# Three rounded products for the branch and attention output layers, with a new order of the conv transfers

## The reference

```python
# block 1, first layer: a causal convolution over time, 31 taps per channel
u = a * sigmoid(gate)                       # of h @ w_pw1
u = conv(u, w_dw) + b_dw                    # depthwise
u = silu(layer_norm(u)) @ w_pw2 + b_pw2
# block 2, end: two attentions with 8 heads of 64 each, gated, and two output layers
y_a = o_a * silu(z_a);  y_b = o_b * silu(z_b)
m = sigmoid(gate_a) * (y_a @ w_a) + sigmoid(gate_b) * (y_b @ w_b)     # "branch"
x = x + rms_norm(m @ w_o)                                             # "w_o2"
# block 3, middle: three mixers, each with an output layer, then a common one
merged = sigmoid(g_a) * ya + sigmoid(g_b) * yb + sigmoid(g_c) * yc    # ya, yb, yc: "outs3"
x = x + merged @ w_o                                                  # "w_o3"
```

## Time and profile before

| | |
|---|---|
| runs | 2034.17, 2035.84, 2044.3 us; median 2035.84 |
| profiled execution | 2035.59 us, span 2033.8 us, mean granted clock 0.994 |
| TensorE | 1986.1 us busy, 98% of the span |
| VectorE, ScalarE, POOL | 1494.9, 1187.3, 58.1 us busy |
| DMA | 510.23 MB, mean 251 GB/s; some 370 GB/s in the experts' stage |

### The profile page before, as it was taken

One profiled execution on the slowest core, in us unless ns is written; L12 is line 12 of the kernel. 1 busy time (PEld: TensorE's weight loads), 2 busy tenths in 40 slices (PEclk: granted clock), 3 DMA queues, 4 the chain that ended last, 5 costly groups with the idle time before them and its releaser, 6 DMA issues.

```text
span 2033.8 us, 31638 instructions
## 1 busy us (share of the span) xinstructions
PE 1986.1 (98%) x12238; PEld 1738.0 (85%) x12238; DVE 1494.9 (73%) x1623; ACT 1187.3 (58%) x1264; POOL 58.1 (3%) x105
## 2 busy tenths in 40 slices
PE   8999999999999999999999999999989999999997
PEld 7689999688888888888888888889978879989997
DVE  7766554789989999999899999977484358536652
ACT  4254443778777787777778777773354355325442
POOL 3020000000000000000000000010000000020000
PEclk9999999999999999999999999999999999999999
DMA  6625453399999999999999999974523334445551
GB/s 241 182 104 178 175 196 136 124 359 373 360 372 362 366 371 354 371 365 365 363 366 374 357 372 363 366 272 167 186 84 108 127 116 147 166 145 187 186 183 48
DMA packets 75863, 510.23 MB, mean 251 GB/s; under 512 B 8320, under 2 KB 14464, under 8 KB 14592
## 3 DMA queue, kind: packets, MB, share of 16 engines
q1 hardware_dynamic: 75776, 508.98, 67.4%
HBM read 506.66 MB, written 2.29 MB: 250 GB/s over the span
## 4 chain that ended last, share of the span: by engine, by line
PE 87%; DVE 4%; DMA 3%; issue 2%; ACT 2%; SPq 1%; POOL 0%; ACTq 0%; DVEq 0%; POOLq 0%
PE ps L904 9%; PE ps L908 9%; PE ps L907 9%; PE ps L638 8%; PE ps L641 8%; PE ps L642 8%; PE ps L929 5%; PE ps L933 5%; PE ps L932 5%; PE ps L615 3%; DMA spread<-big 2%; PE ps L1195 2%; PE ps L1198 2%; PE ps L1197 2%; PE ps L1130 1%
## 5 line engine op out<-in xcount | busy, mean ns | idle before, releaser
L1896 DVE TENSOR_TENSOR ring_r<-ring,high 128x2048 fp32r<-128x2048 f32 x227 | 517.6, 2288 | 55.0 <-ACT high L1566 34.0
L1566 ACT ACTIVATE high<-ring 128x2048 fp32r<-128x2048 f32 x224 | 428.8, 1914 | 19.1 <-DMA ring<-w_stream 18.5
L1781 DVE TENSOR_TENSOR ring_r<-ring,high 128x2048 fp32r<-128x2048 f32 x120 | 274.6, 2292 | 128.2 <-ACT high L1379 128.0
L907 PE MATMUL ps<-ring_r,big_r 128*128 128x512 f32 x896 | 349.2, 390 | 0.0
L641 PE MATMUL ps<-scr_r,high 128*128 128x256 f32 (+1 forms) x1200 | 342.7, 286 | 0.0
L1379 ACT ACTIVATE high<-ring 128x2048 fp32r<-128x2048 f32 x120 | 228.2, 1908 | 165.0 <-PE ps L638 93.3
L1896 DVE TENSOR_TENSOR ring_r<-ring,scr_r 128x2048 fp32r<-128x2048 f32 x112 | 256.3, 2288 | 39.6 <-ACT scr_r L1566 39.1
L638 PE MATMUL ps<-sq_r,high 128*128 128x272 f32 (+1 forms) x832 | 238.4, 287 | 5.4 <-DVE scr_r L1788 5.4
L642 PE MATMUL ps<-sq_r,ring_r 128*128 128x272 f32 (+1 forms) x832 | 237.9, 286 | 0.0
L1566 ACT ACTIVATE scr_r<-ring 128x2048 fp32r<-128x2048 f32 x112 | 214.5, 1915 | 22.5 <-DMA ring<-w_stream 22.4
L641 PEld LDWEIGHTS ps<-scr_r,high 128*128 128x128 f32 x1200 | 227.2, 189 | 0.3
(11 more groups left out here) (482 smaller groups left out, 3779.0 us busy)
## 6 DMA issues: line engine op xcount, KB each, us to landing
ring<-w_stream SPq DMA_DIRECT2D x477, 1024.0 KB, 4.8
big<-spread SPq DMA_DIRECT2D x32, 146.0 KB, 2.9
spread<-big SPq DMA_DIRECT2D x8, 151.0 KB, 6.1
h<-h_in SPq DMA_DIRECT2D x1, 1088.0 KB, 5.1
out<-hn SPq DMA_DIRECT2D x1, 1024.0 KB, 4.7
vec<-vec_in SPq DMA_DIRECT2D x1, 576.0 KB, 8.1
```

Of the source, the lines that this page charges most:

```text
L907: pe.matmul(o, x_item_high[:, k, :], w_low[:, cols], start=False, stop=False)
L1566: act.activation(w_high, w, ACT.Copy).then_inc(S["moe_high"], 1)
L1781: dve.tensor_tensor(w_low, blocks_at(c, 0, CH), w_high.bitcast(F32), ALU.subtract).then_inc(S["weights_low"], 1)
L1896: dve.tensor_tensor(w_low, w, w_high.bitcast(F32), ALU.subtract).then_inc(S["moe_low"], 1)
```

## The change

The convolution: each `shift(j)` of all eight now stands before the chunk 6 + j.

Branch, `w_o2` and `w_o3` join the split stages, 4 chunks each, and their matmuls become three rounded products. The gated attention outputs get a rounded part (`gated_high`, ScalarE, over the used gates in `proj_r`) and a low part (`gated_low`, VectorE, in place), one job after `gated`. ScalarE's sigmoids, and the splits of the first two branch chunks on both engines, move into sub 14. POOL's sums now go to `part` and `part3`; ScalarE copies them into `hn_r`, and VectorE makes the low parts two tiles later, in the loop over m. The splits of the remaining chunks lie between these steps.

```diff
@@ convolution, SP
             for c in range(RING, 3 * RING):
-                if c - RING == KD - 2:
-                    shift(KD - 2)
+                if c - RING < KD:
+                    shift(c - RING)
                 sp.wait_ge(pre_begun, c - RING + 2)
                 sp.dma_start(slot(c), w_stream[c]).then_inc(dense_landed[c % RING], 16)
-                if c - RING < KD - 2:
-                    shift(c - RING)
-                if c - RING == KD - 2:
-                    shift(KD - 1)
@@ TensorE, branch
-                        mm = pe.matmul(ps[:, 2 * (j % 2) + 4 * br + half, 0:SEQ], w[:, half * P:half * P + P],
-                                       sq256[:, 4 * br + k, :], start=(k == 0), stop=(k == 3))
+                        mm = pe.matmul(o, w_high[:, cols], proj_r[:, z + k, :], start=(k == 0), stop=False)
                         begun(half == 0 and first, mm)
+                        pe.matmul(o, w_high[:, cols], sq_r[:, 4 * br + k, 0:SEQ], start=False, stop=False)
+                        mm = pe.matmul(o, w_low[:, cols], proj_r[:, z + k, :], start=False, stop=(k == 3))
...
-                    pe.wait_ge(S["y_ready"], 4)
+                    pe.wait_ge(S["input_low"], 8 * 4 + 4)
                     branch(0)
...
-            pe.wait_ge(S["y_ready"], 8)
+            pe.wait_ge(S["input_low"], 8 * 4 + 8)
...
-                pair(BOFF["w_o2"] + j * KD, KD, lambda k: hn256[:, k, :], SEQ, b, S["wo2_done"],
-                     (lambda k: pe.wait_ge(S["br_ready"], k + 1)) if j == 0 else None)
+                split_pair(BOFF["w_o2"] + j * KD, KD, hn_r, in_low, SEQ, b, S["wo2_done"],
+                           after_split(5) if j == 0 else None)
...
-                pair(BOFF["w_o3"] + j * KD, KD, lambda k: hn256[:, k, :], SEQ, b, S["wo3_done"],
-                     (lambda k: pe.wait_ge(S["merged"], k + 1)) if j == 0 else None)
+                split_pair(BOFF["w_o3"] + j * KD, KD, hn_r, merged_low, SEQ, b, S["wo3_done"],
+                           after_split(7) if j == 0 else None)
@@ ScalarE, attention
+            def gated_high(j):
+                act.wait_ge(S["y_ready"], j + 1)
+                whole, high_part, _ = gated_parts(j)
+                act.activation(high_part, whole, ACT.Copy).then_inc(S["input_high"], 1)
...
                     exps(s + 2)
+                if s >= 2 and subs[s - 2][0] != subs[s - 1][0]:
+                    gated_high(subs[s - 2][0])
                 split_weights(chunk2(merge_pairs_done(s) - 1 + LOOK))
-            for p in merge_order:
...
+                if s == len(subs) - 2:
+                    split_weights(BOFF["branch"] // CH + 1)
+                    for p in merge_order:
+                        act.wait_ge(S["in2_dve"], p + 1)
+                        dst, _ = tiles2(p)
+                        act.activation(dst, dst, ACT.Sigmoid).then_inc(S["in2_act"], 1)
+            split_weights(BOFF["branch"] // CH + 2)
+            gated_high(len(jobs) - 2)
+            gated_high(len(jobs) - 1)
+            split_weights(BOFF["branch"] // CH + 3)
             for m in range(KD):
+                act.wait_ge(S["br_ready"], m + 1)
+                act.activation(hn_r[:, m, 0:SEQ], part[:, m % 2, 0, :], ACT.Copy).then_inc(S["input_high"], 1)
+                if m in (1, 3, 5):
+                    split_weights(BOFF["w_o2"] // CH + m // 2)
@@ ScalarE, block 3
             curved(PAIRS3 - 1, ACT.Sigmoid)
+            split_weights(BOFF["w_o3"] // CH + 2)
+            for m in range(KD):
+                act.wait_ge(S["merged"], m + 1)
+                act.activation(hn_r[:, m, 0:SEQ], part3[:, m % 2, 0, :], ACT.Copy).then_inc(S["input_high"], 1)
+                if m == 1:
+                    split_weights(BOFF["w_o3"] // CH + 3)
@@ VectorE, attention
                 while taken2 < merge_pairs_done(s):
                     take2(taken2)
                     taken2 += 1
+                if s == len(subs) - 2:
+                    split_weights(BOFF["branch"] // CH + 1)
+                if s >= 2 and subs[s - 1][0] != subs[s - 2][0]:
+                    gated_low(subs[s - 2][0])
             gated(len(jobs) - 1)
+            gated_low(len(jobs) - 2)
+            gated_low(len(jobs) - 1)
+            split_weights(BOFF["branch"] // CH + 2)
@@ VectorE, branch sums
                 if m >= 2:
-                    dve.wait_ge(S["br_ready"], m - 1)
+                    low_part(in_low[:, m - 2, :], part[:, m % 2, 0, :], hn_r[:, m - 2, 0:SEQ], "input_low")
+                    dve.wait_ge(S["input_low"], 8 * 5 + m - 1)
...
+                if m == 1:
+                    split_weights(BOFF["branch"] // CH + 3)
+                if m in (3, 5):
+                    split_weights(BOFF["w_o2"] // CH + m // 2 - 1)
@@ VectorE, block 3
+            split_weights(BOFF["w_o3"] // CH + 1)
             dve.wait_ge(S["mh_ready"], 1)
             for m in range(KD):
...
                 if m >= 2:
-                    dve.wait_ge(S["merged"], m - 1)
+                    low_part(merged_low[:, m - 2, :], part3[:, m % 2, 0, :], hn_r[:, m - 2, 0:SEQ], "input_low")
+                    dve.wait_ge(S["input_low"], 8 * 7 + m - 1)
+                if m in (2, 4):
+                    split_weights(BOFF["w_o3"] // CH + m // 2 + 1)
```

More of the change, by code:

```diff
@@ L101 @@
 assert len(MOE_ORDER) == MOE_CH
-SPLIT_STAGES = ("pw1", "pw2", "ffn0_in", "ffn0_out", "w_in2a", "w_in2b0", "w_in2b", "w_in3", "ffn3_in", "ffn3_out")
+SPLIT_STAGES = ("pw1", "pw2", "ffn0_in", "ffn0_out", "w_in2a", "w_in2b0", "w_in2b", "branch", "w_o2", "w_in3", "w_o3", "ffn3_in", "ffn3_out")
 SPLIT_ALL = [c for _name, _n in STAGES if _name in SPLIT_STAGES
@@ L291, in program, with gated_parts @@
         sq256 = sq[:, :, 0:SEQ]
+        merged_low = proj_r[:, 0:8, :]
+        def gated_parts(j):
+            kind, i, hh = jobs[j]
+            z, at = (ZA, 0) if kind == "nsa" else (ZB, 4)
+            q = slice(i * P, (i + 1) * P)
+            whole = sq256[:, at + 2 * hh:at + 2 * hh + 2, q]
+            return whole, proj_r[:, z + 2 * hh:z + 2 * hh + 2, q], sq_r[:, at + 2 * hh:at + 2 * hh + 2, q]
         hn256 = hn[:, :, 0:SEQ]
@@ L1181, in half_pair @@
                     if p == 0 and half == 0:
-                        pe.wait_ge(S["input_low"], 8 * 4 + k + 1)
+                        pe.wait_ge(S["input_low"], 8 * 6 + k + 1)
                     if half == 0:
@@ L2226, in gated, with gated_low @@
                                   proj[:, z + 2 * hh:z + 2 * hh + 2, q], ALU.mult).then_inc(S["y_ready"], 1)
+            def gated_low(j):
+                whole, high_part, low = gated_parts(j)
+                low_part(low, whole, high_part, "input_low")
             biased(0)
@@ L2254, in _ @@
                 ins.then_inc(S["br_part"], 1)
+                if m == 1:
+                    split_weights(BOFF["branch"] // CH + 3)
+                if m in (3, 5):
+                    split_weights(BOFF["w_o2"] // CH + m // 2 - 1)
+            for m in (6, 7):
+                low_part(in_low[:, m, :], part[:, m % 2, 0, :], hn_r[:, m, 0:SEQ], "input_low")
             split_weights(BOFF["w_in3"] // CH + 2)
@@ L2423, in _ @@
                 ins.then_inc(S["out3_part"], 1)
+            for m in (6, 7):
+                low_part(merged_low[:, m, :], part3[:, m % 2, 0, :], hn_r[:, m, 0:SEQ], "input_low")
             for m in range(KD):
@@ L2534, in _ @@
                 pool.wait_ge(S["br_part"], m + 1)
-                pool.tensor_tensor(hn256[:, m, :], part[:, m % 2, 0, :], part[:, m % 2, 1, :], ALU.add)\
+                pool.tensor_tensor(part[:, m % 2, 0, :], part[:, m % 2, 0, :], part[:, m % 2, 1, :], ALU.add)\
                     .then_inc(S["br_ready"], 1)
```

16 lines of the change are left out of this document (9 added, 7 removed).

## The result

The changed kernel takes 2050.65 us in the median of 8 runs (2040.88 to 2052.34), the kernel before 2034.61 us in the median of 8 beside it. The ratio is 1.0072 (95% interval 1.0055 to 1.0088): slower by 0.7%, where I had forecast 2039 and no difference. The profiled execution of the changed kernel took 2040.88 us, with a span of 2039.1 and a mean granted clock of 0.994. It is the shortest of the 8. The other seven have mean clocks of 0.986 to 0.991 and take 2047.05 to 2052.34. This matters for all that follows: the profiled execution of after is 5.3 us longer than that of before (2035.59), but the medians lie 16 us apart.

The account below looks back on a forecast made before the run. The prediction took TensorE to bound the kernel nearly throughout. On the profiled 2035.6 us, -14.8 + 1.2 + 5.9 + 4.3 + 6.9 = +3.5 gave 2039 us, likely range 2033 to 2045, with bounds at one end 2025 and 2049.

Parts of the forecast that it names:

- Part 1: Branch, w_o2 and w_o3: three rounded products in place of each of 192 fp32 matmuls save TensorE 14.8 us.
- Part 2: Convolution: chunk 11 ahead of spread 6 delays tiles 6 and 7, partly returned by the clock; +1.2 us, bounds 0 and 3.9.
- the conv order does what it looks like: Rival, convolution: every spread goes free of weights and tile 7 waits no longer; -5 us, so 2033; chance 0.08.
- Part 3: Attention: VectorE waits for ScalarE's gated copies at four subs and TensorE pays; +5.9 us, bounds 1 and 9.
- Part 4: End of attention: TensorE idles 3.8 us for the first branch chunk's low part; +4.3 us of waits, bounds 1 and 6.
- Part 5: Before and in outs3: TensorE waits 2.8, 1.3 and 2.8 us behind weight splits; +6.9 us, bounds 2 and 9.
- the new idles drop the clock: Rival: half clock behind new idles at branch 0, in outs3 and conv tile 7; +14 us, 2050 us; chance 0.17.
- so nothing has to be shifted between the two: Whole kernel before: profiled execution 2035.6 us and median 2035.8, so the sum made on the profile needs no shift.
- is close to neither row: outs3: its 2.8 us idles lie near neither the 4.41 us that dropped the clock nor the 1.70 that did not.
- the granted clock falls in new places: Sign, anywhere in the kernel: if the clock falls where it did not before, the sum is wrong.
- The rival of absorbed waits: Attention and outs3: most new waits are hidden; -5.5 us, 2030, or 2024 to 2026 at the deepest; chance 0.20.

Follow-up runs that it names:

- e4: The kernel before with only the new order of the conv transfers: 2036.81 us, ratio 1.0004.
- e1: The changed kernel run once more, unchanged: 2050.69 us, ratio 1.0079.
- e2: The changed kernel with the old order of the conv transfers put back: 2043.23 us, ratio 1.0024.
- e11: The changed kernel with gated low parts later, splits of w_o3 and first branch chunks and sigmoids earlier, new conv order kept: 2032.17 us, ratio 0.9998.
- e8: The changed kernel with gated low parts later, splits of w_o3 and first branch chunks and sigmoids earlier, old conv order: 2025.66 us, ratio 0.9965.
- e3: The changed kernel with unread filling matmuls in TensorE's new waits before branch 0 and in outs3: 2042.76 us, ratio 1.0026.
- e16: The changed kernel with the old conv order and filling matmuls before branch 0 and in outs3: 2040.43 us, ratio 1.0028.
- e5: The changed kernel with VectorE's low part of a gated attention job taken one loop step later: 2041.48 us, ratio 1.0046.
- x_tail_order: The changed kernel with the first branch chunk split earlier, the second behind the sigmoids on ScalarE and in sub 15 on VectorE: 2042.99 us, ratio 1.0054.
- e6: The changed kernel with the splits of w_o3 set earlier on ScalarE and VectorE: 2042.75 us, ratio 1.0047.
- e13: The changed kernel, unchanged, profiled again as the first of three looks: 2040.68 us.
- e15: The changed kernel, unchanged, profiled again as the third of three looks: 2052.29 us.

## Why the prediction was wrong

**Part 1, products: right.** `w_o3` takes 22.9 us of TensorE's timeline in after where fp32 took 27.8: 4.9 us, as forecast for each of the three layers. `w_o2` gives the same 4.9. TensorE's busy time fell by 14.5 us of the 14.8.

**Part 2, conv order: a loss, as forecast, but not by the forecast steps.** `spread` 6 took 5.75 us, and not 3.57; I had put 7.1. The forecast moved tile 6 by 4 us; it moved by 0.4, because `spread` 5 went out 3.1 us sooner than before (73.56, not 76.70) and covered for it. The wait before tile 7 grew to 5.89 instead of going away, and of the 2.7 us that the clock was to give back on tile 7 came 1.2 (4.42 us against 5.63). Over all profiled executions the last filling matmul behind the conv starts at 119.2 us with the new order (12 of them, 117.4 to 122.4) and at 117.2 with the old (6, 113.8 to 122.4): 2 us with a scatter of several, inside the bounds 0 and 3.9. By the ratios the new order costs 0.8 us (e4), 11 (e1 against e2), 6.7 (e11 against e8) and -0.4 (e3 against e16). The mean of those four is 4.5 us, above the bounds. The clock is in them. In time times mean clock, averaged over the runs, the same four comparisons give 3.1, 2.4, 3.4 and 0.9 us. The rival "the conv order does what it looks like" is out.

**Part 3, gated parts: right.** 5.35 us of waits in the four places against 5.9, and undoing it gave 5.9 in the profile (e5).

**Part 4, end of attention: the idle is right.** It is 3.80 us against 3.8. The sum of 4.3 was not measured by itself; 2.9 us could be had by reordering (x_tail_order).

**Part 5, `outs3`: right.** 2.37, 1.26 and 3.09 us against 2.8, 1.3 and 2.8; 6.7 against 6.9.

**The sum was +3.5 us, and the profiled execution shows +5.3.** That the two are so close is in part luck. From the first row of L1126 (L1119 in the kernel before) that reads `h` to the end, after takes 552.9 us and before took 546.6: +6.3, where parts 1, 3, 4 and 5 make +2.3. Ahead of that row after is 1.0 us sooner, where part 2 made it 1.2 later. Of the 4.0 us too many in the tail, 3.4 are the two new drops; the profile of before had one of its own there, at 1710.7, which the one of after hasn't.

**The step that failed** is that the sum has no term for the clock behind the new idles. It was left to the first of the rivals, "the new idles drop the clock", with a chance of 0.17. With it fails a sentence ahead of the parts, "so nothing has to be shifted between the two". Against the rival I wrote that 2.8 us "is close to neither row", that TensorE is dense on both sides, and that between 1.70 and 4.41 us the trace shows nothing. The last was not so. The timeline of TensorE of the kernel before has an idle of 3.90 us ahead of its first weights, and the clock of 17 to 21 us is 0.59:

```profile
17.33 0.37 PE L638 MATMUL ps<-sq_r,high 128*128 128x272 f32 x1 [3.90 <-DVE scr_r L1788]
```

```profile
17.00:21.00 4.00, 3.67 (x18) 3.70 (x18) 2.82 (x6) 2.55 (x3) 1.72 (x3) 0.59 1.02 424
```

An idle of that length stands there in all 18 profiles, with a drop each time. So a drop behind part 4's 3.8 us was to be expected, and all nine profiles with that idle (3.2 to 3.8 us) have it. Behind part 5's idles the runs show less order: 2.37 us is followed by full clock in one execution and by half clock in the next, 3.0 to 3.2 us by half clock in all nine. And the 2.16 us that part 3 makes in sub 13 is followed by half clock in five of eleven.

What it came to is in the mean granted clocks of all runs: 0.9925 to 0.9942 for the kernel before in the four sessions, 0.9888 and 0.9872 for after in two. In the session of e1_again the difference is 0.0053, and 0.0053 of 2040 us are 11 us. In time times clock after lies 3.8 us above before in that session (95% interval 1.4 to 6.2), where the sum said 3.5. This takes all time to stretch with the clock, which waits do not, so it is an estimate. By it the terms for work and waits were right together, and nearly all of what was missed is clock. The prediction had named "the granted clock falls in new places" as a sign that its sum is wrong.

The evidence that the idles are the cause is e3_fill with e16_conv_old_fill. Both take away no wait and add work in them, and both have the mean clock of the kernel before (0.9924 against 0.9925, 0.9927 against 0.9928). The rival's 2050 agrees with the median partly by luck. It added up twice the time for one branch, two tiles of `outs3` and conv tile 7; in the profiled execution the two drops cost 3.4 us, and in the slow ones part of the loss lies elsewhere. One profiled execution could not show this, in either kernel, and the spread of three runs (2034 to 2044) was a warning that I took for noise.

The rival of absorbed waits is out: every wait stood where its row put it.

**What stays open.** Filling the idles and restoring the conv order each gained about 11 us by the ratios, yet no more together. With the filling the mean clock is that of the kernel before in both builds, so the order has no clock left to give back there; that fits, but why the old order raises the clock without the filling (0.9872 to 0.9899) is not shown. Nor do I know what makes the drops near 1635 and 1715, which the kernel before has too. The three single reorderings gained 6.7, 6.5 and 5.1 us against e1_again by the ratios, where the waits and drops they took away come to 5.9 us, 7.7 us (`outs3` takes 22.4 us in e6's timeline, 30.2 in that of after) and, for the end of attention, nearly nothing in the profile. Intervals of 0.0015 to 0.0028 to each side don't separate these. And why a given execution keeps its clock through the same idles is not told by any run here. The Trainium skill, page "TensorE: Matmul & The Clock Gate", section "What's actually happening", says that the monitor behind the gate runs freely and isn't reset by the start of a kernel, so that one kernel shows different numbers of slow matmuls from run to run. e13 and e15 agree: one program, mean clocks of 0.993 and 0.986. The same section holds the penalty of the ramp to be under 1% of a typical span and advises against fitting a count of slow matmuls. Here the difference in mean clock was 0.5%, and that was most of what the change lost.

## What to carry to other kernels

A microsecond of TensorE's waiting is not worth a microsecond of its work: in this kernel idles of 2 to 4 us cost their length and, in some or in all of the executions, 1.7 us and more of clock behind each. When work is split over several engines to make TensorE's part cheaper, first set the helpers' steps so early that no new stop appears (here that turned a ratio of 1.0079 into 0.9998, and 0.9965 with the old conv order); where a stop must stay, filling it can pay (e3_fill: from 1.0079 to 1.0026). And set the sum against the spread of the runs and their clocks, not against the one execution that was profiled.

## What the runs showed of the hardware that I had not expected

- A stage with TensorE busy 6.00 of 6.00 us ran at a granted clock of 0.50 in three of the fifteen profiled executions without filling there (e2_conv_old, e3_fill, e6_outs_order), and at 1.00 in the other twelve. Its matmuls are small: one kind fills 8 columns of the array, the other streams 31 to 113 columns. With two full matmuls ahead of each step it stayed at full clock in all three profiles (router stage 18.2 us each time), but that is 7.0 us more work, as much as the drop costs where there is one.
- The kernel before ranged from 2026.15 us at a clock of 0.997 to 2046.28 at 0.989, over all sessions. At equal clock the runs agree better: time times mean clock averages 2021 us in each of its four sessions, and over all 96 runs its standard deviation is 2.2 us where that of the time is 4.6.
- With the idle of 3.80 us cut to 0.78, the clock stayed at 1.00 behind it (1563 to 1570 us), but fell for longer behind an idle of 2.84 us, 12 us later (x_tail_order).
- TensorE dropped to half clock near 1715 us in ten of 18 profiled executions, the kernel before among them, though it was busy 12.00 of the 12.00 us from 1708 to 1720.
